# A decoder layer on one core: half of the contraction with w_out by seven block products of eight

## What is computed

```python
merged = (sigmoid(gate_att) * (y_att @ w_branch_att)
          + sigmoid(gate_dn) * (y_dn @ w_branch_dn))
y = merged @ w_out
x = x + rms_norm(y, post_norm_mix)
h = rms_norm(x, pre_norm_mlp)
x = x + rms_norm(square(relu(h @ w_mlp_in)) @ w_mlp_out, post_norm_mlp)
```

## Time and profile before

| | us |
|---|---|
| median of 3 runs | 753.74 (753.39 to 754.31) |
| the profiled execution | 753.69 |
| its span, from the first to the last instruction | 751.9 |

### The profile page before, as it was taken

How to read it: one execution, slowest core, us unless ns; L and a number is a source line. 1 busy time by engine, 2 the same in 40 slices (tenths; PEclk the granted TensorE clock), 3 DMA queues, 4 the chain that set the end, 5 groups by cost and what they waited for, 6 DMA issues and landing times.

```text
span 751.9 us, 12181 instructions
## 1 busy us (share of the span) xinstructions
PE 744.5 (99%) x4180; PEld 610.3 (81%) x4180; DVE 418.1 (56%) x627; ACT 383.9 (51%) x623; POOL 322.6 (43%) x294
## 2 busy tenths in 40 slices
PE   9999999999999999999999999999999999999996
PEld 7788778888877878788887988888888888888885
DVE  5796899980444545345702612211221777788795
ACT  6656842268554365635524833323332655555671
POOL 2357894435454754575446464445445000000002
PEclk9999999999999999999999999999999999999999
DMA  9336224577596688397941244556484775554652
GB/s 329 112 88 208 56 65 117 156 183 173 165 196 156 188 176 210 100 224 211 287 160 42 71 126 141 130 183 168 129 214 129 202 237 189 194 191 159 208 183 113
DMA packets 83214, 123.45 MB, mean 164 GB/s; under 512 B 5824, under 2 KB 44896, under 8 KB 83168
## 3 DMA queue, kind: packets, MB, share of 16 engines
q1 hardware_dynamic: 74384, 105.80, 43.9%
q0 software_dynamic: 8448, 16.78, 13.1%
q10 hardware_dynamic: 336, 0.28, 0.1%
HBM read 120.73 MB, written 35.67 MB: 208 GB/s over the span
## 4 chain that ended last, share of the span: by engine, by line
PE 93%; POOL 3%; ACT 2%; DVE 1%; issue 0%; ACTq 0%; POOLq 0%; DVEq 0%
PE bank L676 28%; PE bank L678 27%; PE bank L677 27%; POOL rsq L1955 2%; PE bank L901 1%; PE bank L924 1%; PE bank L911 1%; POOL w_lo L1961 1%; PE bank L865 1%; PE bank L829 1%; PE bank L697 1%; PE bank L706 1%; PE bank L876 1%; PE bank L933 1%; PE bank L973 0%; PE bank L703 0%
## 5 line engine op out<-in xcount | busy, mean ns | idle before, releaser
L1961 POOL TENSOR_TENSOR w_lo<-raw,w_hi 128x512 fp32r<-128x512 f32 x177 | 229.5, 1305 | 251.5 <-ACT w_hi L1113 249.7
L1113 ACT ACTIVATE w_hi<-raw 128x512 fp32r<-128x512 f32 (+2 forms) x214 | 144.9, 684 | 171.7 <-PE bank L678 160.1
L676 PE MATMUL bank<-h_hi,w_hi 128*128 128x512 f32 (+1 forms) x528 | 208.5, 395 | 0.1
L677 PE MATMUL bank<-h_lo,w_hi 128*128 128x512 f32 (+1 forms) x528 | 204.2, 387 | 0.0
L678 PE MATMUL bank<-h_hi,w_lo 128*128 128x512 f32 (+1 forms) x528 | 204.1, 386 | 0.0
L676 PEld LDWEIGHTS bank<-h_hi,w_hi 128*128 128x128 f32 x528 | 99.2, 188 | 25.0 <-issue 4.0
L678 PEld LDWEIGHTS bank<-h_hi,w_lo 128*128 128x128 f32 x528 | 99.2, 188 | 20.6
L677 PEld LDWEIGHTS bank<-h_lo,w_hi 128*128 128x128 f32 x528 | 99.3, 188 | 18.7
L1492 DVE SCALAR_TENSOR_TENSOR relu_sb<-bank,rs_row 128x512 f32<-128x512 f32 x32 | 20.6, 686 | 126.5 <-PE bank L678 114.8
L2092 POOL TENSOR_SCALAR ssh<-ssy 128x1 f32<-128x1 f32 x4 | 1.0, 238 | 151.6 <-ACT junk L1463 151.6
L676 PE MATMUL bank<-w_hi,h_hi 128*128 128x512 f32 x128 | 50.3, 393 | 0.1
(11 more groups left out here) (300 smaller groups left out, 1204.2 us busy)
## 6 DMA issues: line engine op xcount, KB each, us to landing
raw<-in_w_in SPq DMA_DIRECT2D x87, 256.0 KB, 3.2
raw<-in_w_mlp_in SPq DMA_DIRECT2D x62, 256.0 KB, 2.7
t_sum<-in_w_mlp_out POOLq DMA_DIRECT2D x12, 1024.0 KB, 10.7
raw<-in_w_mlp_out SPq DMA_DIRECT2D x26, 256.0 KB, 3.0
raw<-t_sum SPq DMA_DIRECT2D x26, 256.0 KB, 3.3
v_sum<-in_w_mlp_out SPq DMA_DIRECT2D x4, 1024.0 KB, 7.1
t_sum<-in_w_mlp_out SPq DMA_DIRECT2D x4, 1024.0 KB, 7.1
v_sum<-in_w_mlp_out POOLq DMA_DIRECT2D x4, 1024.0 KB, 11.5
```

What stands on the lines that cost most here:

```text
L676: pe.matmul(o, s_hi, m_hi, start=start, stop=False, skip_group_check=True)
L677: pe.matmul(o, s_hi, m_lo, start=False, stop=False, skip_group_check=True)
L1113: return a.activation(o, i_, ACT.Copy, scale=scale)
L1961: g.tensor_tensor(w_lo[:, slot, :], raw[:, slot, :], w_hi[:, slot, :].bitcast(F32), ALU.subtract).then_inc(lo_ready, 1)
```

## The change

The rows 0 to 511 of w_out (two groups g of 256) are no longer multiplied block by block. In each group the merged features are taken as a 2 x 2 of blocks (two feature blocks x two halves of the tokens), the weight as a 2 x 2 (two blocks of rows x two halves of the columns), and 7 products of combinations take the place of 8. Rows 512 to 1023 stay plain and come behind it.

- Four combinations of the weight (512 KB each) are made in DRAM like those of w_mlp_out: copies at units 48, 52, 60, 87 and additions two units later. Of the 12 early chunks of w_mlp_out six stay (units 61 to 86); ten run in the MLP's first product, whose loops on SP and POOL are written out.
- DVE multiplies the DeltaNet product by its gate in the bank itself and adds gate_a from there; it then makes four combinations of 128x256 (`differences`), and low parts for them (`o1_low`, `o2_low`).
- PE runs a first sweep of four products per group (`out_one`, 8 units), ACT copies product P1 out of its banks, DVE and ACT form the sums and the seeds of the banks (`x_o`, `y_o`), and a second sweep of three products (`out_two`) is put between the plain blocks.
- The second sweep's weights have their own buffers (`wo_raw`, `wo_hi`, `wo_lo`), loaded by SP in the branch stage and at unit U_BR+6.
- DVE instead of POOL makes the low parts of units U_BR+4 to U_BR+7; the halves of a token tile are squared in another order.

```diff
+OUT_SUM_AT = {48: 0, 52: 1, 60: 2, 87: 3}
+SUM_AT = {61: (0, 0), 65: (1, 0), 73: (2, 0), 74: (0, 1), 78: (1, 1), 86: (2, 1)}
+SUM_IN = {3: (0, 2), 4: (0, 3), 5: (1, 2), 6: (1, 3), 7: (2, 2), 8: (2, 3), 11: (3, 0), 12: (3, 1), 13: (3, 2), 14: (3, 3)}
+OUT_ONE = (("p1", "q5", "p7", "q6"), ("p1", "q6", "p7", "q5"))
+OUT_BANK = {"p1": (4, 6), "q5": (5, 7), "p7": (0, 2), "q6": (1, 3)}
+OUT_TWO = (((4, 6), 1), ((0, 2), 0), ((5, 7), 2))
+U_PLAIN = U_BR + 8
...
SP
+            if u == U_DN + 7:
+                sp_.wait_ge(unit_done, U_DN)
+                sp_.wait_ge(ylo_ready, 2)
+                for e in range(4):
+                    load_out(e)
+            if u == U_BR + 6:
+                sp_.wait_ge(unit_done, U_BR)
+                for e in range(4, 6):
+                    load_out(e)
             if u == U_BR + 4:
-                sp_.wait_ge(ylo_ready, 2)
                 sp_.dma_start(x_res[:], ...).then_inc(xr_in, 16)
...
PE
+        def out_one(g, j):
+            u, s, c = U_BR + 4 * g + j, j, OUT_ONE[g][j]
+            pe.wait_ge(lo_ready, u + 1)
+            if j == 0:
+                pe.wait_ge(olo_ready, g + 1)
+            for i2 in range(2):
+                if g == 0 and c in ("p7", "q6"):
+                    pe.wait_ge(prod_ready, 13 + (c == "q6") + 2 * i2)
+                x_ = three(bank[OUT_BANK[c][i2]][:], o1_hi[...], o1_lo[...], w_hi[:, s, :], w_lo[:, s, :], ...)
+            x_.then_inc(unit_done, 1)
+        def out_two(p):
+            for g in range(OUT_G):
+                e = OUT_G * p + g
+                pe.wait_ge(wolo_ready, e + 1)
+                if p == 0:
+                    pe.wait_ge(olo_ready, OUT_G + g + 1)
+                for i2 in range(2):
+                    three(bank[banks[i2]][:], o2_hi[...], o2_lo[...], wo_hi[e][:], wo_lo[e][:], False, False)
+        for g in range(OUT_G):
+            for j in range(4):
+                out_one(g, j)
+        pe.wait_ge(p1_copied, 2)
+        out_two(0)
+        for t in (2, 3):
+            for j in range(4):
+                pe.wait_ge(mlo_ready, j + 1)
+                i = out_part(j, t)
+            i.then_inc(y_done, 1)
+        pe.wait_ge(y_seeded, 2)
+        out_two(1)
+        for j in range(3):
+            out_part(j, 0)
+        out_part(3, 0).then_inc(y_done, 1)
+        for j in range(4):
+            out_part(j, 1).then_inc(unit_done, 1)
+        pe.wait_ge(z_seeded, 2)
+        out_two(2)
+        pe.wait_ge(c22_made, 2)
         for t in range(NT - 1):
+            for j in range(4, 8):
+                i = out_part(j, t)
+            i.then_inc(y_done, 1)
...
ACT, behind split_u(u + LEAD)
+            if u - U_DN in (4, 6):
+                mix_one((u - U_DN) // 2 - 2)
+            if u == U_DN + 7:
+                for g in range(OUT_G):
+                    mix_two(g)
+            if u == U_BR:
+                for e in range(2):
+                    split_out(e)
+            if u in (U_BR + 1, U_BR + 3):
+                for m in range(2):
+                    k = u - U_BR - 1 + m
+                    a.wait_ge(prod_ready, 13 + k)
+                    mark(copy(h_hi[:, 4 + k, :], m_a[:, k, :]), mhi_ready)
+            if u == U_BR + 5:
+                for i2 in range(2):
+                    copy(x_o[:, i2, :], bank[4 + 2 * i2][:]).then_inc(p1_copied, 1)
+            if u == U_BR + 7:
+                for e in range(2, 4):
+                    split_out(e)
...
DVE
+        def gated(g):
+            v.wait_ge(gates_ready, 8 + 2 * g + 2)
+            v.wait_ge(unit_done, U_DN + 2 * g + 2)
+            for m in range(2):
+                b = bank[g % 2 * 2 + m][:]
+                link(v.tensor_tensor(b, b, gate_d[:, 2 * g + m, :], ALU.mult))
+                mark(v.tensor_tensor(mixed(g, m), b, gate_a[:, 2 * g + m, :], ALU.add), prod_ready)
+        def m_low(k):
+            v.wait_ge(mhi_ready, k + 1)
+            mark(v.tensor_tensor(h_lo[:, 4 + k, :], m_a[:, k, :], h_hi[:, 4 + k, :].bitcast(F32), ALU.subtract), mlo_ready)
+        gated(0)
+        differences(0)
+        gated(1)
+        differences(1)
+        o1_low(0)
+        gated(2)
+        o1_low(1)
+        gated(3)
+        v.wait_ge(lo_ready, U_BR + 4)
+        for u in range(U_BR + 4, U_BR + 7):
+            out_low(u)
+        o2_low(0)
+        out_low(U_BR + 7)
+        o2_low(1)
+        m_low(0)
+        m_low(1)
+        for i2 in range(2):
+            v.wait_ge(p1_copied, i2 + 1)
+            v.wait_ge(unit_done, U_BR + 6)
+            mark(v.tensor_tensor(x_o[:, i2, :], bank[1 + 2 * i2][:], x_o[:, i2, :], ALU.subtract), x_made)
+        for i2 in range(2):
+            v.wait_ge(unit_done, U_BR + 7)
+            v.tensor_tensor(y_o[:, i2, :], x_o[:, i2, :], bank[2 * i2][:], ALU.subtract).then_inc(y_made, 1)
+        m_low(2)
+        m_low(3)
...
POOL
+        for u in range(U_DN + LEAD, U_BR + 4):
+            split_u(u)
+        out_low(0)
+        out_low(1)
+        g.wait_ge(lo_ready, U_PLAIN)
+        for u in range(U_PLAIN, U_PLAIN + 4):
+            split_u(u)
+        for e in range(2, 6):
+            out_low(e)
+        for u in range(U_PLAIN + 4, U_OUT):
+            split_u(u)
```

More of the change, by code:

```diff
@@ L1297, in _ @@
                     mark(a.activation(gate_d[:, 2 * g + m, :], gate_d[:, 2 * g + m, :], ACT.Sigmoid), gates_ready)
-            if u - U_DN in (3, 5, 7, 9):
-                g = (u - U_DN - 3) // 2
-                for m in range(2):
[L1301 to L1313, removed]
+            if u - U_DN in (4, 6):
+                mix_one((u - U_DN) // 2 - 2)
+            if u == U_DN + 7:
+                for g in range(OUT_G):
[4 more added lines that the diff above has]
+            if u in (U_BR + 1, U_BR + 3):
+                for m in range(2):
+                    k = u - U_BR - 1 + m
[7 more added lines that the diff above has]
+                    split_out(e)
+            if u == U_PLAIN:
+                for i2 in range(2):
+                    a.wait_ge(y_made, i2 + 1)
+                    a.activation(bank[2 * i2][:], y_o[:, i2, :], ACT.Copy, scale=-1.0).then_inc(y_seeded, 1)
+                for e in range(4, 6):
+                    split_out(e)
+                square_y(4)
+                square_y(6)
+                square_y(0)
         def square_x2(t):
@@ L1735, in _, with mixed @@
                 side_step(name, i)
-        for g in range(4):
+        def mixed(g, m):
+            return m_mix[g][:, 5 * m:5 * m + 2, :].rearrange("p a c -> p (a c)") if g < OUT_G else m_a[:, 2 * g + m - 4, :]
+        def gated(g):
             v.wait_ge(gates_ready, 8 + 2 * g + 2)
@@ L1749, in _, with scaled @@
+        for i2 in range(2):
+            v.wait_ge(unit_done, U_BR + 8)
+            v.tensor_tensor(bank[1 + 2 * i2][:], y_o[:, i2, :], bank[5 + 2 * i2][:], ALU.add).then_inc(c22_made, 1)
+        for i2 in range(2):
+            v.tensor_tensor(bank[5 + 2 * i2][:], x_o[:, i2, :], bank[5 + 2 * i2][:], ALU.add).then_inc(z_seeded, 1)
         v.wait_ge(xr_in, 16)
         v.wait_ge(pn_in, 32)
-        def scaled(t, pn, s0):
-            for half in range(2):
+        def scaled(t, pn, halves=range(2)):
+            for half in halves:
@@ L1772, in _ @@
         for t in range(2):
-            scaled(t, pn_mix, 0)
+            scaled(t, pn_mix, (0,))
+        for t in range(2):
+            scaled(t, pn_mix, (1,))
             residual(t)
@@ L2075, in _ @@
         root_x2()
[L2076 to L2086, removed]
+        for u in range(U_OUT + 6, U_M1):
             split_u(u)
+            if (u - U_OUT) % 4 == 1 and (u - U_OUT) // 4 - 1 in SUM_IN:
+                q, i = SUM_IN[(u - U_OUT) // 4 - 1]
+                g.wait_ge(t_copied[q], 16 * (i + 1))
+                g.dma_start(*t_add(q, i), accum_op=ALU.add).then_inc(t_added[q], 16)
         def root_end(t, first_, second):
```

206 lines of the change are left out of this document (139 added, 67 removed).

## The result

The changed kernel takes 757.61 us (median of 6 runs, 756.39 to 758.28), the kernel before 753.68 beside it: a ratio of 1.0049, 95% interval 1.0039 to 1.0060. It is slower by 3.9 us, where 754.8 was forecast with a range up to 756.7.

The account below looks back on a forecast made before the run. TensorE (PE), busy 99% of the span, was taken as the bound. The terms -2.72 - 0.45 + 0.2 + 3.1 + 1.0 gave +1.1 us on 753.69, so 754.8 us, with a range of 751.2 to 756.7.

Parts of the forecast that it names:

- The mechanism: In the w_out stage, DVE operations with two SBUF operands stand still while POOL runs, ending 0.54 us behind POOL's.
- Rival 1: In the w_out stage DVE is not held by POOL, waits are 0.9 us at most: 751.4 us; chance 0.18.
- the sum: All terms of the w_out stage added up, +1.1 us on the profiled 753.69, giving 754.8.
- the load: Weight U_BR+5 of the first sweep, needed earlier, lands at 375.3, so PE starts it 0.2 us late.
- the two m_low waits: PE waits in token tile 2's plain blocks 2 and 3 for m_low(2) and m_low(3): 3.1 and 1.0 us.
- the breaks regained: Of 1.05 us of PE breaks in the old w_out stage, 0.45 us were counted as going away.
- the missing addition: POOL's 1 MB addition, in the DMA engines until 366.6 before, is gone there; up to 2.6 us earlier landing for U_BR+5.
- Rival 2: U_BR+5's load lands as late as before, 378.3; PE waits 3.2 us at the sixth weight: 757.8; chance 0.07.
- The matmuls: The w_out stage has 180 matmuls in place of 192, 12 fewer at 0.227 us: 2.72 us less.
- Rival 3: Moved combinations overfill the DMA in the MLP's first product; PE could wait some 2 us: 756.8; chance 0.06.
- PE at 369.92: Sign: PE reaching the w_out stage later than 369.92 would mean a gated sum holds a branch product up.
- The edits counted at no cost: Gated sums from a bank, lighter early DMA, unrolled SP and POOL loops cost nothing while PE is last to arrive.

Follow-up runs that it names:

- low_first: Against the changed kernel, DVE makes m_low(2) and m_low(3) right behind m_low(1), ahead of the x and y differences; 754.34 us.
- pool_waits: Against the changed kernel, POOL waits for the last m_low before making low parts of the four last second-sweep weights; 755.04 us.
- load_by_weight: Against the changed kernel, x_res and both norms are issued behind unit U_BR+11 and PE takes plain blocks 0 to 3 weight by weight; 750.10 us.

## Why the prediction was wrong

- **The mechanism was right.** PE breaks for m_low(2), released by DVE's h_lo, held beside POOL's w_lo and wo_lo; low_first and pool_waits show both halves. Rival 1 (DVE is not held) is out: 3.48 against 1.41 us. Each h_lo ended 0.55 us behind POOL's operation, as worked out from the earlier trace rows (0.54). That the one behind blocks, as the Trainium skill has it (SBUF — State Buffer, Who interferes with whom), agrees with these ends.
- **The step that failed is the sum.** It priced a break at its own length and put the clock behind it at nothing. Behind the long one PE ran 14 steps at half clock: 3.06 us in this profile, 1.6 (8 x 0.2) in the second one. The stage's +4.34 against the forecast +1.13 are +3.06 for the half clock, +1.47 for the load with the pace behind it, -1.11 for the two m_low waits and -0.21 for the breaks regained. The PEclk column of the earlier trace rows is 1.00 throughout, as the kernel before had no such break; a forecast of 3 us of standstill should have asked what the clock does then.
- **The load was mis-sized:** 0.2 forecast, 1.45 measured (2.07 in the second profile, 1.63 to 2.53 in the four others with the same loads ahead). I had it land at 375.3; it landed at 377.1 (issued 367.87, and 9.2 us). The 3.67 MB were priced at the 417 GB/s of a stretch of 4 us. Over the whole transfer, windows of the changed kernel give 366:
```profile
366.00:377.10 11.10, 11.10 (x50) 8.89 (x48) 9.32 (x11) 6.12 (x10) 6.94 (x5) 1.00 1.01 366
...
366.00:368.00 2.00, 2.00 (x11) 1.65 (x9) 1.97 (x3) 0.86 (x2) 1.84 (x1) 1.00 0.92 243
368.00:372.00 4.00, 4.00 (x19) 3.33 (x18) 3.86 (x6) 3.38 (x6) 2.06 (x2) 1.00 1.02 420
372.00:374.00 2.00, 2.00 (x11) 1.65 (x10) 1.90 (x4) 1.88 (x4) 2.00 (x3) 1.00 1.03 328
```
420 GB/s are reached, but not kept, and more than the 3.67 MB moved: 4.24 MB from the issue of U_BR+4 at 364.39 to the landing, 0.57 of them for loads issued behind. How the delay splits between the two, no run shows. Of the 2.6 us that the missing addition was to give back, some 1.5 came (378.3 to 377.1, and 0.35 for the later start). By the 358 GB/s of the Trainium skill (DMA: Bandwidth & Descriptors, Specifications) the landing was an estimated 376.1, the nearer one; as a limit the figure is not borne out, since single windows lie above it. Rival 2's landing (378.3) was 1.2 us off on the other side, and its break of 3.2 us at the sixth weight came in no profile; its 757.8 is near the measured time for another reason, the clock, and so by luck.
- **The two m_low waits:** 3.1 and 1.0 forecast, 2.76 and 0.23 measured. DVE's whole chain ran 1.6 us later than worked out (m_low(2) at 389.7, not 388.1), and PE 1.9 us (at the end of block 1, 387.0, not 385.05), both by the load and by the 0.35 us of the later start. The wait for m_low(3) was hidden by the slow matmuls of block 2 (389.73 to 391.41); in the second profile, where that block ran at full clock, it was 0.90.
- **The matmuls and the breaks regained:** -2.72 holds. Of the 1.05 us, 0.66 went and not 0.45. load_by_weight shows both: a stage of 42.92 us (369.82 to 412.74).
- **Rival 3** did not happen in the changed kernel (160.00 of 160.00 us busy). The two single breaks are of its kind, PE waiting for a weight's low part, but no median moved with them.
- **PE at 369.92:** it came at 370.27, which by my last sentence would mean that a gated sum holds a branch product up. It does not: between 10 and 370 PE has no break over 0.15 us. The first matmul with a weight begins at 5.05 (before at 4.89), the first pairs go at other paces in the two executions, and the difference is 0.32 us from 20 on and 0.35 from 150 on, long before the gated sums.
- The edits counted at no cost (gated sums in the bank, lighter early DMA) cost nothing, by the same absence of breaks.

What stays open is which breaks take the clock down: 2.53 us with none ahead of it did not, 2.58, 2.76 and 2.84 with a shorter one some ten us ahead did, 2.04 behind such a one did not in its profile, 3.15 alone did, and 3.67 alone did not in its profile, though by their times and clocks it did in the three executions beside it.

## What to carry to other kernels

A saved matmul is worth its time only while nothing else arrives later than PE, and a standstill of PE is not priced by its length alone: the granted clock behind it cost as much again here (3.06 us behind 2.76), so the longest break is the first to remove, even by reordering PE's own work. A load behind megabytes is to be sized with the mean rate over the whole transfer, not with the best stretch, and with the loads that are issued behind it in mind. When three small orders (SP's issue, DVE's list, PE's loop) meet in one place, try each alone before the change is given up: here two of them turned 3.9 us lost into more than 3 gained.

## What the runs showed of the hardware

- Half clock came in stretches of 7, 8 or 14 steps, most of them of 0.43 us, and could begin after PE had resumed: in the second profile of the changed kernel the first three matmuls behind 2.84 us ran at full pace, and the slow ones began at 392.25, behind the 0.90 us break.
- POOL pays too: of the four w_lo in the 6.59 us from 381.31 on, the three beside DVE operations with two SBUF operands took 1.94, 1.63 and 1.74 us, the fourth, beside operations with a bank, 1.29.
- The start of an execution varies by more than a small edit: the same stage began at 369.54 to 372.34 in these profiles. In the latest (pool_waits) PE waited 0.94 us for its first weight, and until 10.3 us its pairs of matmuls took 0.85 us in place of 0.46.
